# A two-block transformer on one core: five input transfers reordered, and a mixer's windowed means moved from VectorE to TensorE

## The chip, the cores and the metric

The kernel runs on one core of a Trainium2 chip. The metric is the time of one execution in device microseconds (us), the median of several runs. All data is fp32; TensorE does each fp32 matmul as two records of the profile ("x16" there is eight matmuls).

## What is computed

256 tokens of width 1024 (and 256 context tokens) pass through a first block of two layers and then a second block of two layers. The change touches two places: the very first norm (`rms_norm` of all 512 tokens with a modulation computed from `c`), and the mixer of each of the second block's two layers. There, one projection `u @ w_in` is split into attention (q, k, v), an indexer (qi, ki, wi) that selects keys, a gated convolution and a pooling:

```python
u = jnp.einsum('bsd,de->bse', a, w_in[i])
q, k, v, qi, ki, wi, u_conv, u_pool = jnp.split(u, IN_SPLITS, axis=-1)
y_attn = dsa_sparse_attention(q, k, v, qi, ki, wi)     # relu(qi.ki)*wi summed over 16 heads, top 64 keys
y_conv = conformer_conv(u_conv, ...)                   # 31 taps, layer norm, silu, 256x256 product
y_pool = multiscale_pool(u_pool, pool_w[i], pool_scale[i])
...
def multiscale_pool(u, pool_w, pool_scale):            # 4 groups of 64 columns, windows 2, 4, 8, 16
    for gi, w in enumerate(POOL_WINDOWS):
        win_sum = c[:, :, sl] - c_pad[:, POOL_PAD - w:POOL_PAD - w + S, sl]   # c: running sum over tokens
        outs.append(win_sum / count - uf[:, :, sl])    # causal mean minus the token itself
    y = jnp.einsum('bsgc,gcd->bsgd', y, pool_w)
    return y * pool_scale
```

## The kernel before

Every engine runs one straight program, written out stage by stage; semaphore counters order them. **Weights** are one stream of 128x128 blocks in the exact order of use, in chunks of 16 blocks (1 MB), which SyncE's queue loads into a ring of five chunks (`weight_ring`): a chunk is issued when the last use of the chunk five before it is done, and TensorE waits for a chunk's arrival once (`K.arrived`). `weight_blocks` lays the stream out, `next_blocks` books it.

**Start.** ScalarE's queue issues, in this order, the vectors, the tokens (`residual`, 2 MB), the first constants, `decay_rows` (32 numbers broadcast to 128 partitions) and `position_row` (256 integers broadcast). `have` waits for all of them. `first_norm` squares the eight token tiles on ScalarE (L666), TensorE sums them with a matrix of ones (L658), ScalarE takes the root (L668), VectorE the reciprocal (L680), multiplies (L683) and applies gain and shift (L691, with ScalarE's L675). Beside it TensorE computes the first modulation (L621) in eight steps, one chunk each: four before the sums, four behind. ScalarE's `rest_of_constants` then issues the other constants. The even mixer follows (L1877, L1885); `decay_rows` is read there at L1983 and L2069, and `position_row` only in the second block.

**Mixer of the second block (`sparse_mixer`).** TensorE projects 22 tiles one after another (`project(m)`, L2539, weights stationary; for wi and v the tokens are stationary, L2533), ping-pong between banks 0 and 1; ScalarE copies each out (`take`). Between tiles TensorE runs `rotate` (rotary products, L2545), `dots` (L2556), the sums of the layer norm (L2562, L2568), and at the end `small` (L2578 the convolution's product, L2582 the pooling's). VectorE's order is: `convolve` (L2685 to L2691), `pool_windows` (L2702 to L2709), rotary steps `rope(0)`, `rope(1)`, `centre`, `rope(2)`, two `add`, `rope(3)`, two `add`, `rope(4)`, four `add`, `select(0)`, `normalise`, `select(1)` (top-64 by repeated maximum), `rope(5)`, `rope(6)`, `rope(7)` (each L2717 to L2719). TensorE's `rotate(7)` waits for `rope(5)` because both use bank 7, and `small` stands behind it. The attention stage (first L761) waits for the masks, all rotary steps, v and `small`'s outcome (L2675, L2677); GpSimd's weight sums for the output projection wait for the same.

Of the kernel before, what the change touches and what calls it, by code (L numbers as in the profile page):

```python
# [16 lines left out]
ALU = mybir.AluOpType  # L17
# [75 lines left out]

def weight_blocks(x):
# [29 lines left out]
    for i in range(2):  # L124
# [3 lines left out]
        out.append(pack_tiles(w, columns(256, o[7])))  # L128
        out.append(pack_rows(w, [list(range(o[5], o[5] + 16)) + [-1] * 112]))
        out.append(pack_tiles(w, [list(range(o[4], o[4] + 64)) * 2]))  # L130
        out.append(pack_tiles(w, columns(1024, o[3])))
        out.append(pack_tiles(w, paired(0)))
        out.append(pack_tiles(w, columns(128, o[1])))
        out.append(pack_rows(w, columns(128, o[2])))
# [4 lines left out]
        out.append(np.stack([pool[:P, :P], pool[P:, P:]]))  # L139
        rows = np.concatenate([np.arange(512, 1024)] + [np.array(t) for t in paired(0)])  # L140
# [35 lines left out]
def constant_parts():  # L176
# [34 lines left out]
    w = np.array([2, 4, 8, 16])  # L211
    c["pool_count"] = np.stack([1.0 / np.minimum(t + 1, w[2 * n + (np.arange(P) // 64)][:, None]) for n in range(2)], 1)
# [432 lines left out]
def first_norm(K, h, piece, gains, gain, shift, out, tokens_ready, rest_of_constants):  # L645
# [1200 lines left out]
def even_projections(K, R, u, k_ready, qkvT, gate, qd, kvd, kpe, ktok, vtok, pads, conv, narrow, low_squares):  # L1846
# [109 lines left out]
    def scalar(act):  # L1956
# [25 lines left out]
        act.activation(narrow, ab[:, :, 64:96], ACT.Copy).then_inc(sg["e_narrow"].sem, 1)  # L1982
        act.activation(ea, R.rows[:, 0:16], ACT.Exp).then_inc(sg["e_rows"].sem, 1)  # L1983
# [49 lines left out]
    def vector(dve):  # L2033
# [34 lines left out]
        dve.tensor_scalar(x[:, :, 16:32], ab[:, :, 16:32], -1.0, None, ALU.mult)  # L2068
        dve.tensor_tensor(out=x[:, :, 0:16], in0=ab[:, :, 0:16], in1=bc(R.rows[:, 16:32], 1, 4), op=ALU.add).then_inc(sg["e_shifted"].sem, 1)  # L2069
# [406 lines left out]
def sparse_mixer(K, R, layer, u, deps, k_ready, ahead):  # L2476
# [9 lines left out]
    ppad = area.get(2, 16 + S)  # L2486
# [5 lines left out]
    sums = [area.get(2, 16 + S) for _ in range(4)]  # L2492
# [13 lines left out]
    needs = [8] + [tiles.index(("qi", i + 1)) + 1 for i in (0, 2, 4, 6)] + [tiles.index(("q", i + 1)) + 1 for i in (0, 2)] + [21]  # L2506
# [5 lines left out]
              "in_normed": 1, "in_active": 1, "in_small": 1, "in_small_out": 1, "in_masks": 1}  # L2512
    sg = {n: K.counter(n) for n in counts}
    at = {n: sg[n].reserve(c) for n, c in counts.items()}
    first = [K.next_blocks(KT, (sg["in_product"], at["in_product"] + m + 1)) for m in range(len(tiles))]
    small_first = K.next_blocks(6, (sg["in_small"], at["in_small"] + 1))

# [3 lines left out]
    def tensor(pe):  # L2521
        need(pe, deps)

        def project(m):
# [3 lines left out]
            if name in ("wi", "v"):  # L2528
# [41 lines left out]

        def small():
            pe.wait_ge(sg["in_active"].sem, at["in_active"] + 1)
            pe.wait_ge(sg["in_taken"].sem, at["in_taken"] + len(tiles))
# [11 lines left out]
        for m in range(len(tiles)):  # L2585
            project(m)
            if m == 12:
                rotate(0)
                rotate(1)
            elif m == 13:  # L2590
# [4 lines left out]
            elif m == 14:  # L2595
                dots(0)
                dots(1)
                pe.wait_ge(sg["in_centred"].sem, at["in_centred"] + 1)
                rotate(3)
            elif m == 15:  # L2600
                dots(2)
                dots(3)
                pe.wait_ge(sg["in_roped"].sem, at["in_roped"] + 3)
                variance()
            elif m == 16:
# [4 lines left out]
            elif m == 17:  # L2610
                dots(6)
                dots(7)
            elif m == 20:
                pe.wait_ge(sg["in_root"].sem, at["in_root"] + 1)
                rotate(5)
                pe.wait_ge(sg["in_roped"].sem, at["in_roped"] + 5)
                rotate(6)
        pe.wait_ge(sg["in_roped"].sem, at["in_roped"] + 6)
        rotate(7)
        small()  # L2620

    def scalar(act):
        act.wait_ge(sg["in_cleared"].sem, at["in_cleared"] + 1)

        def take(m):
# [7 lines left out]
            elif name == "p":  # L2633
                ins = act.activation(ppad[:, i, 16:], ps, ACT.Copy)
# [16 lines left out]
        for m in range(len(tiles)):  # L2651
            take(m)
            if m == 14:
# [4 lines left out]
            elif m == 15:  # L2658
                rectify(2)
                rectify(3)  # L2660
# [438 lines left out]
```

## Time and profile before

| | us |
|---|---|
| median of 3 runs | 2283.7 (2282.51 to 2284.52) |
| the profiled execution, own time | 2289.73 |
| its span, first to last instruction | 2287.6 |
| PE (TensorE matmul) busy | 2184.0 (95%) |
| PEld (TensorE weight load) busy | 1519.8 (66%) |
| DVE (VectorE) busy | 1061.5 (46%) |
| ACT (ScalarE) busy | 459.4 (20%) |
| POOL (GpSimd) busy | 139.7 (6%) |
| mean granted TensorE clock | 0.983 of full |
| read from HBM | 280.12 MB, 123 GB/s over the span |

Read it by stage: TensorE is busy nearly always, so what counts are the few places where it stands idle or runs at the lower clock. A granted clock of 1.00 is 2.4 GHz, 0.50 is 1.2 GHz.

### The profile page before, as it was taken

What the parts mean: (1) busy time and instruction counts of PE and PEld (TensorE: products, weight loads), DVE (VectorE), ACT (ScalarE), POOL (GpSimd) and SP (SyncE); (2) the same over time, 40 slices, a digit from 0 to 9 for tenths busy, and PEclk for the clock granted to TensorE, in tenths of its full rate; (3) what the DMA queues carried; (4) which work ended last, traced back from release to release, by engine and by line L of the source; (5) the groups of instructions that cost most, each with busy time, mean ns of one, the idle gap of its engine ahead of it and who ended that gap; (6) DMA issues with size and microseconds to landing.
All of it is one profiled execution on the core that took longest, in us unless ns stands there. A gap on an engine that the chain in (4) does not pass through costs nothing.

```text
span 2287.6 us, 33060 instructions
## 1 busy us (share of the span) xinstructions
PE 2184.0 (95%) x14140; PEld 1519.8 (66%) x14140; DVE 1061.5 (46%) x1902; ACT 459.4 (20%) x986; POOL 139.7 (6%) x158
## 2 busy tenths in 40 slices
PE   6999999999899999999999999998999999899998
PEld 3447878564588885466567884785785488668646
DVE  2575555461655446652453115675324428632443
ACT  2343211351200000131242000222210111311001
POOL 0003333000000000021100000002000000200000
PEclk9999999999999999999999999999999999999999
DMA  8221444402422224454113444332344433234442
GB/s 324 74 74 39 150 150 153 173 1 74 184 92 92 81 85 148 174 138 128 56 38 120 157 147 176 128 111 74 131 158 172 166 115 124 74 117 159 157 174 74
DMA packets 40799, 283.81 MB, mean 124 GB/s; under 512 B 4944, under 2 KB 6352, under 8 KB 7120
## 3 DMA queue, kind: packets, MB, share of 16 engines
q1 hardware_dynamic: 38480, 273.70, 33.0%
q0 software_dynamic: 1312, 3.15, 1.1%
q10 hardware_dynamic: 864, 4.87, 0.5%
q8 instruction: 113, 1.85, 0.3%
q14 instruction: 30, 0.25, 0.0%
HBM read 280.12 MB, written 1.05 MB: 123 GB/s over the span
## 4 chain that ended last, share of the span: by engine, by line
PE 89%; DVE 7%; ACT 2%; issue 1%; DMA 1%; ACTq 0%; DVEq 0%
PE banks L978 20%; PE banks L405 17%; PE banks L1389 12%; PE banks L1288 7%; PE banks L2539 6%; PE banks L1885 5%; PE banks L1568 2%; PE banks L1592 2%; PE banks L761 1%; PE banks L1588 1%; PE banks L621 1%; PE banks L443 1%; PE banks L776 1%; PE banks L493 1%; PE banks L767 1%
## 5 line engine op out<-in xcount | busy, mean ns | idle before, releaser
L405 PE MATMUL banks<-normed,weight_ring 128*128 128x256 f32 (+1 forms) x1280 | 294.9, 393 | 7.8 <-DVE normed L557 5.7
L405 PEld LDWEIGHTS banks<-normed,weight_ring 128*128 128x128 f32 x1280 | 244.9, 192 | 57.2 <-issue 15.3
L978 PE MATMUL banks<-arena 128*128 128x512 f32 x360 | 171.0, 593 | 0.7 <-DVE arena L1444 0.5
L1288 PE MATMUL banks<-normed,weight_ring 128*128 128x256 f32 x704 | 153.8, 382 | 3.4 <-ACT normed L571 3.4
L2539 PE MATMUL banks<-normed,weight_ring 128*128 128x256 f32 x640 | 151.4, 399 | 5.8 <-DVE normed L557 2.9
L1288 PEld LDWEIGHTS banks<-normed,weight_ring 128*128 128x128 f32 x704 | 134.8, 192 | 22.4 <-ACT normed L571 3.8
L978 PE MATMUL banks<-weight_ring,arena 128*128 128x512 f32 x322 | 149.2, 592 | 0.0
L2539 PEld LDWEIGHTS banks<-normed,weight_ring 128*128 128x128 f32 x640 | 128.0, 201 | 26.9 <-issue 4.6
L978 PEld LDWEIGHTS banks<-arena 128*128 128x128 f32 x360 | 68.2, 190 | 87.5 <-issue 86.1
L1885 PE MATMUL banks<-normed,weight_ring 128*128 128x512 f32 x288 | 126.1, 593 | 0.0
L978 PEld LDWEIGHTS banks<-weight_ring,arena 128*128 128x128 f32 x322 | 60.9, 190 | 73.1 <-issue 72.9
L3005 DVE TENSOR_TENSOR arena<-arena 128x256 f32<-128x256 f32 x64 | 27.2, 425 | 171.3 <-ACT arena L2993 170.6
L943 DVE TENSOR_TENSOR arena<-weight_ring 128x512 f32<-128x512 f32 x59 | 40.7, 690 | 141.1 <-PE banks L978 141.1
L1885 PEld LDWEIGHTS banks<-normed,weight_ring 128*128 128x128 f32 x288 | 54.3, 190 | 66.7 <-issue 66.7
L1389 PE MATMUL banks<-normed,weight_ring 128*128 128x256 f32 x352 | 82.9, 390 | 6.8 <-ACT normed L571 4.3
L1389 PEld LDWEIGHTS banks<-normed,weight_ring 128*128 128x128 f32 x352 | 68.8, 196 | 18.1 <-issue 5.1
L1441 DVE TENSOR_TENSOR arena<-squares,banks 128x512 f32<-128x512 f32 x22 | 15.1, 687 | 132.1 <-ACT squares L1417 132.1
L1015 ACT ACTIVATE branch<-banks 128x512 f32<-128x512 f32 x8 | 4.8, 598 | 336.6 <-PE banks L978 336.6
L1306 DVE TENSOR_TENSOR arena<-banks,arena 128x256 f32<-128x256 f32 x22 | 9.3, 424 | 131.4 <-PE banks L1288 127.1
L621 PE MATMUL banks<-weight_ring,silu_cond 128*32 128x512 f32 x384 | 54.2, 650 | 16.3 <-DMA weight_ring<-in_weights 7.3
L835 DVE TENSOR_REDUCE attention_small<-banks 128x1 f32<-128x512 f32 (+2 forms) x96 | 48.0, 530 | 45.5 <-PE banks L767 41.1
L815 ACT ACTIVATE arena<-banks,attention_small 128x512 f32<-128x512 f32 (+2 forms) x96 | 54.0, 563 | 60.3 <-DVE attention_small L835 60.3
(464 smaller groups left out, 3432.6 us busy)
## 6 DMA issues: line engine op xcount, KB each, us to landing
weight_ring<-in_weights SPq DMA_DIRECT2D x260, 1024.0 KB, 4.8
constants<-in_const ACTq DMA_DIRECT2D x1, 2209.5 KB, 13.9
residual<-in_tokens ACTq DMA_DIRECT2D x1, 2048.0 KB, 12.6
mix<-in_rpb POOLq DMA_DIRECT2D x32, 64.0 KB, 3.6
out<-residual SPq DMA_DIRECT2D x1, 1024.0 KB, 4.8
branch<-arena POOLq DMA_DIRECT2D x1, 512.0 KB, 4.9
normed<-in_ple POOLq DMA_DIRECT2D x1, 512.0 KB, 3.7
vector_params<-in_vectors ACTq DMA_DIRECT2D x1, 223.0 KB, 5.6
```

Of the source, the lines that this page charges most:

```text
L405: mm = pe.matmul(K.psum[lo:hi, banks[m % nb], 0:T], K.block(first[m] + k)[:, lo:hi], rhs(k), start=(k == 0), stop=(k == n_k - 1))
L621: mm = pe.matmul(o, self.silu[:, k, :], self.K.block(self.first[k] + 4 * j, 4), start=(k == 0), stop=(k == KT - 1))
L815: act.activation(prob[:, i % 4, 0:x.n], K.bank(i % 4, x.n), ACT.Exp, bias=maximum[:, i % 4:i % 4 + 1], accum_out=total[:, i % 4:i % 4 + 1] ...
L835: dve.reduce_max(maximum[:, i % 4:i % 4 + 1], K.bank(i % 4, rounds[r].n), AX, negate=True).then_inc(sg["maxima"].sem, 1)
L943: dve.tensor_tensor(out=t3, in0=b22, in1=b12, op=ALU.subtract)
L978: return pe.matmul(self.bank[i], left, b, start=(p == 0), stop=(p == n - 1))
L1288: mm = pe.matmul(K.bank(i % 4, T), K.block(first[i] + k), u[:, k, 0:T], start=(k == 0), stop=(k == KT - 1))
L1389: mm = pe.matmul(self.outs(p)[i], a[:, k * P:k * P + P], right(k), start=(k == 0), stop=(k == H - 1))
L1568: mm = pe.matmul(heads(2 * u)[halves[n], m, :], L[u][lv % 2][halves[n], m, :], X[u][halves[n], m, :], start=True, stop=True)
L1592: mm = pe.matmul(heads(2 * u + 1)[halves[n], m, :], PR[u][halves[n], m, :], Y[u][halves[n], m, :], start=True, stop=True)
L1885: mm = pe.matmul(K.bank(f % 4), K.block(first[f] + k), u[:, k, :], start=(k == 0), stop=(k == KT - 1))
L2539: mm = pe.matmul(K.bank(m % 2, S), K.block(first[m] + k), u[:, k, 0:S], start=(k == 0), stop=(k == KT - 1))
```

## The change

1. *Start.* `decay_rows` and `position_row` are issued behind the rest of the constants, and `have` counts two transfers fewer. ScalarE and VectorE wait for them (and all constants) before L1983 and L2069. The modulation's steps are split three before the sums and five behind.
2. *Pooling.* `pool_windows`, its padded tiles, their memsets and the constant `pool_count` go. The two p tiles are projected with tokens stationary, so that they come out by token, and TensorE multiplies them by banded 128x128 matrices (causal mean minus identity) that stand in the weight stream (`window_blocks`, 12 blocks a layer; the zero upper right block is not stored). ScalarE copies the result out.
3. *Order.* The p tiles move behind the qi tiles; `rotate`, `dots` and the layer norm's sums move to earlier tiles; `small` moves ahead of the v tile, so v moves behind the pooling's weights in the stream; `rope(5)` moves ahead of `select(1)`.

The stream has 262 chunks, not 260. The diff, cut to its core:

```diff
+def window_blocks():
+    i, j = np.arange(S)[:, None], np.arange(S)[None]
+    for w in (2, 4, 8, 16):
+        m = ((i <= j) & (i > j - w)) / np.minimum(j + 1, w) - (i == j)
+        out += [m[:P, :P], m[:P, P:], m[P:, P:]]
...
     def tensor(pe):                       # first_norm
-        piece.product(pe, 0, 4)
+        piece.product(pe, 0, 3)
...
-        piece.product(pe, 4, KT)
+        piece.product(pe, 3, KT)
...
+        need(act, K.constants_ready)
         act.activation(ea, R.rows[:, 0:16], ACT.Exp).then_inc(sg["e_rows"].sem, 1)
...
+        need(dve, K.constants_ready)
         dve.tensor_tensor(out=x[:, :, 0:16], in0=ab[:, :, 0:16], in1=bc(R.rows[:, 16:32], 1, 4), op=ALU.add)
...
-    tiles = [("a", 0), ("a", 1), ("g", 0), ("g", 1), ("p", 0), ("p", 1), ("wi", 0), ("ki", 0)] + [("qi", i) for i in range(8)] \
+    tiles = [("a", 0), ("a", 1), ("g", 0), ("g", 1), ("wi", 0), ("ki", 0)] + [("qi", i) for i in range(8)] + [("p", 0), ("p", 1)] \
         + [("q", i) for i in range(4)] + [("k", 0), ("v", 0)]
...
-            if name in ("wi", "v"):
+            if name in ("wi", "v", "p"):
...
+        def windows():
+            pe.wait_ge(sg["in_taken"].sem, at["in_taken"] + tiles.index(("p", 1)) + 1)
+            pe.wait_ge(sg["in_relu"].sem, at["in_relu"] + 8)
+            for g in range(4):
+                rows, m = slice(64 * (g % 2), 64 * (g % 2) + 64), g // 2
+                o = K.psum[rows, 5, m * S:m * S + S]
+                for at_block, (t, lo, stop) in enumerate(((0, 0, True), (0, P, False), (1, P, True))):
+                    K.arrived(pe, window_first + 3 * g + at_block)
+                    mm = pe.matmul(o[:, lo:lo + P], ptok[:, m, t, rows], K.block(window_first + 3 * g + at_block), start=(at_block < 2), stop=stop)
+            mm.then_inc(sg["in_meaned"].sem, 1)
...
+            elif m == 19:                 # scalar
+                act.wait_ge(sg["in_meaned"].sem, at["in_meaned"] + 1)
+                act.activation(z.rearrange("p m n -> p (m n)"), K.bank(5), ACT.Copy).then_inc(sg["in_pool"].sem, 1)
...
         convolve()
-        pool_windows()
         rope(0)
...
         normalise()
+        rope(5)
         select(1).then_inc(sg["in_masks"].sem, 1)
-        rope(5)
         rope(6)
...
         def rest_of_constants(act):
-            act.dma_start(K.const[:, n_first:], const[:, n_first:]).then_inc(constants_loaded.sem, 16)
+            for dst, src in ((K.const[:, n_first:], const[:, n_first:]), (R.rows, rows.to_broadcast([P, 32])), (R.positions, positions.to_broadcast([P, S]))):
+                act.dma_start(dst, src).then_inc(constants_loaded.sem, 16)
-        have = [(loaded, 16 * 4)] + have_vectors
+        have = [(loaded, 16 * 2)] + have_vectors
```

TensorE at the end of a mixer, before: the last three projected tiles by weights (q2, q3, k), `rotate(5)` and `rotate(6)`, v, `rotate(7)`, and `small` ahead of the attention.

```order
L2539 MATMUL banks<-normed,weight_ring 128x256 x24
L2545 MATMUL banks<-arena,constants 128x256 x4
L2533 MATMUL banks<-weight_ring,normed 128x128 x16
L2545 MATMUL banks<-arena,constants 128x256
L2578 MATMUL banks<-branch,weight_ring 128x256 x4
L2582 MATMUL banks<-branch,weight_ring 128x256 x2
L761 MATMUL banks<-arena 128x128 x2
```

The same place after the change; L2592 is `windows`, L2601 and L2605 are `small`, L2546 is v.

```order
L2558 MATMUL banks<-arena,constants 128x256 x2
L2552 MATMUL banks<-normed,weight_ring 128x256 x8
L2592 MATMUL banks<-weight_ring,arena 64x128 x12
L2552 MATMUL banks<-normed,weight_ring 128x256 x8
L2558 MATMUL banks<-arena,constants 128x256 x2
L2601 MATMUL banks<-branch,weight_ring 128x256 x4
L2605 MATMUL banks<-branch,weight_ring 128x256 x2
L2546 MATMUL banks<-weight_ring,normed 128x128 x16
L2558 MATMUL banks<-arena,constants 128x256
L770 MATMUL banks<-arena 128x128 x2
```

`small` now stands ahead of v and of the last rotary product, and twelve window matmuls are new.

VectorE around `normalise`, before: the end of `select(0)`, the reciprocal and product of `normalise`, then the first step of `select(1)`.

```order
L2750 TENSOR_SCALAR arena<-arena 128x128
L2751 TENSOR_TENSOR arena<-arena,constants 128x128
L2742 RECIPROCAL inverses<-roots 128x256
L2743 TENSOR_TENSOR branch<-branch,inverses 128x512
L2748 MAX arena<-arena 128x8
```

After the change, at the same place:

```order
L2764 TENSOR_SCALAR arena<-arena 128x128
L2765 TENSOR_TENSOR arena<-arena,constants 128x128
L2756 RECIPROCAL inverses<-roots 128x256
L2757 TENSOR_TENSOR branch<-branch,inverses 128x512
L2731 TENSOR_TENSOR arena<-banks,mix 128x512
L2732 TENSOR_TENSOR arena<-arena,mix 128x512
L2733 TENSOR_TENSOR arena<-arena 128x512
L2762 MAX arena<-arena 128x8
```

The three instructions of `rope(5)` have come in ahead of `select(1)`.

## Rows read from the trace of the kernel before

**Rows 1.** Waits of PE, second mixer (1800 to 1990 us): waiting line <- releaser: us, times, longest

```profile
PE banks L2545 <- DVE arena L2719: 6.8, 1, 6.8
```

**Rows 2.** The chain, 0 to 130 us: start, us, what

```profile
2.89 20.19 DMA position_row<-in_positions
...
23.10 0.64 ACT normed L666
...
23.79 8.94 PE banks L658 x16
...
43.11 11.45 PE banks L1877 x64
...
76.38 0.36 PE banks L1898 x4
```

**Rows 3.** DMA issues, 0 to 80 us: size, us from issue to landing

```profile
constants<-in_const ACTq DMA_DIRECT2D x1, 2209.5 KB, 13.9
...
constants<-in_const ACTq DMA_DIRECT2D x1, 128.5 KB, 15.0
```

**Rows 4.** Timeline, 0 to 130 us: start, us, what, idle before

```profile
1.67 0.45 ACTq L2839 DMA_DIRECT2D constants<-in_const  x1
...
16.51 1.93 PE L621 MATMUL banks<-weight_ring,silu_cond 128*32 128x512 f32 x8 [0.94 <-DMA weight_ring<-in_weights]
...
32.64 3.64 PE L621 MATMUL banks<-weight_ring,silu_cond 128*32 128x512 f32 x32
...
37.00 0.66 PE L634 MATMUL banks<-constants,roots 128*128 128x128 f32 x4 [0.72 <-ACT roots L629]
...
56.25 0.21 ACT L1983 ACTIVATE gates<-decay_rows 128x16 f32<-128x16 f32 x1
...
66.00 0.23 DVE L2074 SCALAR_TENSOR_TENSOR gates<-gates 128x64 f32<-128x64 f32 x1
```

**Rows 5.** Stretches: us, PE, PEld, DVE, ACT, POOL busy; clock, DMA, GB/s

```profile
30.00:32.00 2.00, 2.00 (x6) 0.93 (x5) 0.00 (x0) 0.00 (x0) 0.00 (x0) 1.00 0.98 410
...
48.00:50.00 2.00, 2.00 (x12) 2.00 (x11) 0.00 (x0) 0.00 (x0) 0.00 (x0) 0.50 0.96 398
...
200.00:400.00 200.00, 192.52 (x5302) 160.11 (x5302) 106.44 (x165) 40.76 (x67) 78.33 (x70) 1.00 0.37 136
```

**Rows 6.** Timeline of PE, first mixer of the second block

```profile
1471.98 4.38 PE L2533 MATMUL banks<-weight_ring,normed 128*128 128x16 f32 x32
...
1541.42 3.73 PE L2533 MATMUL banks<-weight_ring,normed 128*128 128x128 f32 x32
1551.91 1.22 PE L2545 MATMUL banks<-arena,constants 128*128 128x256 f32 x2 [6.76 <-DVE arena L2719]
...
1559.01 0.49 PE L761 MATMUL banks<-arena 64*128 64x128 f32 x4 [1.51 <-ACT mix L2677]
```

**Rows 7.** The chain, same mixer: tile pitch, `small`, a 64-column product

```profile
1476.36 23.42 PE banks L2539 x96
...
1501.08 3.45 PE banks L2539 x16
...
1553.14 3.41 PE banks L2578 x8
...
1561.54 0.37 PE banks L785 x4
```

**Rows 8.** Timeline of DVE, same mixer

```profile
1494.67 0.72 DVE L2702 TENSOR_TENSOR branch<-arena 128x542 f32<-128x542 f32 x1
...
1499.41 0.69 DVE L2709 TENSOR_TENSOR branch<-branch,arena 128x512 f32<-128x512 f32 x1
...
1540.71 0.69 DVE L2743 TENSOR_TENSOR branch<-branch,inverses 128x512 f32<-128x512 f32 x1
...
1549.51 0.43 DVE L2751 TENSOR_TENSOR arena<-arena,constants 128x256 f32<-128x256 f32 x1
...
1554.73 0.42 DVE L2719 TENSOR_TENSOR arena<-arena 128x256 f32<-128x256 f32 x1
```

More of the change, by code:

```diff
@@ L131, in weight_blocks @@
         out.append(pack_tiles(w, columns(1024, o[3])))
+        out += [pack_rows(w, columns(128, o[7] + 128 * j)) for j in range(2)]
         out.append(pack_tiles(w, paired(0)))
+        out.append(window_blocks())
         out.append(pack_tiles(w, columns(128, o[1])))
-        out.append(pack_rows(w, columns(128, o[2])))
         out.append(pack_tiles(x["conv_pw_2"][i], columns(256)))
@@ L139, in weight_blocks @@
         out.append(np.stack([pool[:P, :P], pool[P:, P:]]))
+        out.append(pack_rows(w, columns(128, o[2])))
         rows = np.concatenate([np.arange(512, 1024)] + [np.array(t) for t in paired(0)])
@@ L2491, in sparse_mixer @@
     acc, xc = area.get(2, S), area.get(2, S)
-    sums = [area.get(2, 16 + S) for _ in range(4)]
     z = area.get(2, S)
@@ L2505, in sparse_mixer @@
     whole = [ki] + [qi[:, i:i + 2, :] for i in (0, 2, 4, 6)] + [q[:, i:i + 2, :] for i in (0, 2)] + [kk]
-    needs = [8] + [tiles.index(("qi", i + 1)) + 1 for i in (0, 2, 4, 6)] + [tiles.index(("q", i + 1)) + 1 for i in (0, 2)] + [21]
+    needs = [6] + [tiles.index(("qi", i + 1)) + 1 for i in (0, 2, 4, 6)] + [tiles.index(("q", i + 1)) + 1 for i in (0, 2)] + [21]
     turn_bank = [2, 7, 7, 2, 2, 7, 2, 7]
@@ L2511, in sparse_mixer @@
               "in_added": 8, "in_conv": 1, "in_pool": 1, "in_mean": 1, "in_centred": 1, "in_squared": 1, "in_variance": 1, "in_root": 1,
-              "in_normed": 1, "in_active": 1, "in_small": 1, "in_small_out": 1, "in_masks": 1}
+              "in_normed": 1, "in_active": 1, "in_small": 1, "in_small_out": 1, "in_masks": 1, "in_meaned": 1}
     sg = {n: K.counter(n) for n in counts}
     at = {n: sg[n].reserve(c) for n, c in counts.items()}
-    first = [K.next_blocks(KT, (sg["in_product"], at["in_product"] + m + 1)) for m in range(len(tiles))]
+    first = [K.next_blocks(KT, (sg["in_product"], at["in_product"] + m + 1)) for m in range(20)]
+    window_first = K.next_blocks(12, (sg["in_meaned"], at["in_meaned"] + 1))
+    first.append(K.next_blocks(KT, (sg["in_product"], at["in_product"] + 21)))
     small_first = K.next_blocks(6, (sg["in_small"], at["in_small"] + 1))
+    first.append(K.next_blocks(KT, (sg["in_product"], at["in_product"] + len(tiles))))
     def dot_banks(i):
@@ L2694, in convolve @@
             ins.then_inc(sg["in_conv"].sem, 1)
-        def pool_windows():
-            dve.wait_ge(sg["in_taken"].sem, at["in_taken"] + 6)
-            prev = ppad
-            for n, s in enumerate(sums):
-                w = 1 << n
-                lo = 2 * w - 1
-                step(dve.tensor_tensor(out=s[:, :, lo:], in0=prev[:, :, lo:], in1=prev[:, :, lo - w:16 + S - w], op=ALU.add))
-                prev = s
-            count = K.c("pool_count").rearrange("p (m n) -> p m n", m=2)
-            for n, s in enumerate(sums):
-                rows, m = slice(64 * (n % 2), 64 * (n % 2) + 64), n // 2
-                ins = dve.tensor_tensor(out=z[rows, m, :], in0=s[rows, m, 16:], in1=count[rows, m, :], op=ALU.mult)
-            step(ins)
-            dve.tensor_tensor(out=z, in0=z, in1=ppad[:, :, 16:], op=ALU.subtract).then_inc(sg["in_pool"].sem, 1)
         def rope(j):
```

60 lines of the change are left out of this document (28 added, 32 removed).

## The prediction

> **What bounds the kernel now.** I read the page first: TensorE is busy 95% of the span, so the kernel can only gain where TensorE stands idle, runs at the lower clock, or loses work. Then I read, for the two places that the change touches, the chain of waits, and behind it each engine's timeline.
>
> At the start the chain runs through a transfer: `position_row` is issued at 2.89 us, takes 20.19 and so lands at 23.08, and ScalarE's first square starts at 23.10 [rows 2]. The reader should see that what ScalarE needs is there earlier: the first constants are issued at 1.67 [rows 4] and land 15.0 later [rows 3], at 16.67, and the tokens were issued ahead of them. The last 6.4 us are spent on two transfers that nobody reads before 55 us. From the squares on, the chain is fixed work: TensorE's sums from 23.79 to 32.73, then root, reciprocal, multiplies and gains until TensorE starts the even mixer at 43.11 [rows 2].
>
> In each mixer of the second block TensorE works through until v is done (1541.42 + 3.73 = 1545.15), waits 6.76 us for `rope(5)` on VectorE, does `rotate(7)` and `small`, and waits 1.51 us for `small`'s copies; the attention starts at 1559.01 [rows 6]. The second mixer has the same wait of 6.8 us [rows 1]. A hidden third cost stands beside them: behind the wait TensorE runs slowly. The eight records of the convolution's product take 3.41 us, 0.43 each, where the same shape takes 3.45 / 16 = 0.216 in the projections [rows 7]; that is the 1.2 GHz level.
>
> **The start, step by step.** With the two transfers gone from `have`, the squares start at 16.7. TensorE ends the third modulation step at 16.51 + 1.93 = 18.44 [rows 4]; the first square (0.64) is done at 17.3, so the sums start at 18.4, not 23.79: this is why one step was moved behind them. The sums took 8.94 us. At 0.43 for each of 16 records of 512 columns (twice 0.216) they would be 6.9, so before they ran partly at the lower level, after TensorE had been nearly idle. Now they follow 1.93 us of work directly. I take 8.4, with 7.4 and 9.4 as bounds: the end is at 26.8 (25.8 to 27.8) against 32.73, 5.9 us earlier.
>
> The modulation must not become the later of the two paths. Its five remaining steps at 3.64 / 4 = 0.91 us [rows 4] end at 31.4, if chunk 7 is there: eight chunks and 2.4 MB of vectors, tokens and constants are 10.8 MB, and the queue moves 410 GB/s [rows 5], which puts it near 28.5. Before, the copy and the turn took from 32.64 + 3.64 = 36.28 to 37.00 + 0.66 = 37.66 [rows 4], 1.4 us; now they end at 32.8. VectorE's eight multiplies end at about 35.9, so there are 3 us to spare, and the even mixer starts at 43.11 - 5.9 = 37.2. Its first product (64 records, 11.45 us, 0.18 each [rows 2]) ran mostly at 1.2 GHz (granted clock 0.50 at 48 to 50 us [rows 5]) after 5.45 us of idling; now the idling is 4.4 us, and I leave this as it is. Were it all at the upper level, at the 0.117 of v's records below, it would give 4 us more.
>
> What is paid for it: ScalarE and VectorE now wait, ahead of L1983 and L2069, for all constants. These are issued near 32 and land 13.9 us later or somewhat more [rows 3] (one chunk more competes, 0.26 MB of `pool_count` less), at 46 to 48. The two small transfers behind them took 6.4 us before, so they land between 47 and 54. ScalarE comes to L1983 at 56.25 - 5.9 = 50.4. Queued behind it on both engines is the way to the decays, 9.9 us long (56.25 to 66.23 [rows 4]), which TensorE reads at 76.38 [rows 2], now 70.5. Up to 60 the landing costs nothing.
>
> That transfers of 16 and 128 KB take 6.4 us is as the Trainium skill says in "DMA: Bandwidth & Descriptors", Queues, rings and completion order: each engine goes round between its queues packet by packet, so a small transfer waits behind the weights' large packets. The trace agrees (6.4 us for 0.14 MB). By this rule the two meet the weights again in their new place, which is the rival of the late constants below.
>
> **The mixer, step by step.** VectorE loses the pooling, 1494.67 to 1500.10 [rows 8], 5.4 us, and `rope(5)` goes ahead of `select(1)`, which lasts from 1541.40 to 1549.94 [rows 8], 8.5 us. Before, `rope(5)` ended at 1551.9. Now it ends at 1543.4 even if the 5.4 us are all lost in waiting, and near 1538 to 1540 otherwise. Some are lost: VectorE is done with `rope(1)` near 1498, but the mean that `centre` needs stands on TensorE behind thirteen tiles and three rotary products, which end at 1501.08 as before [rows 7]. TensorE reaches `rotate(7)` at 1550.8 (next paragraph), so its wait is gone. What is late next is not VectorE but TensorE's own queue.
>
> I count that from v's end. In front of it come now:
> twelve window matmuls, 24 records of 128 columns on 64 columns of the array. The trace has such records in the attention, four in 0.37 us, 0.093 each [rows 7], and full-width ones in v, 32 in 3.73, 0.117 each [rows 6]. So 2.2 to 2.8; I take 2.5, between the two.
> The two p tiles in v's form: 3.73 - 3.45 = 0.28 each, 0.56.
> `small`, 12 records at 0.216, 2.6.
> The sum is 5.7: v ends at 1545.15 + 5.7 = 1550.8. Then `rotate(7)`, 0.43, and `rope(7)` on VectorE, three instructions of 0.42 [rows 8] and the handover, 1.35, ahead of the attention: 1552.6. The copies of `small` and of the means hide under v (3.73). Against 1559.01 that is 6.4 us. Told as a difference: 6.76 + 1.51 of waits and 2.6 of slow clock (the 14 records from 1551.91 to 1557.50 take 5.6, not 3.0) go, 2.5 + 0.56 of work and 1.35 of a new wait come.
> Two mixers give 12.8; the step to `rope(7)` is handed over on three engines, so I take 12.6.
>
> Bounds. If VectorE won nothing from the dropped sums, `rope(6)` would end as before near 1553.9 and `rope(7)` at 1555.1: 3.9 us a mixer, 7.8 in all. Upwards, windows at the 0.093 and a clock that is never lowered give 7 us, 14 in all.
>
> Free of cost: two chunks more (0.8% of the stream), since the queue can move 410 GB/s [rows 5] and moves 123 on the mean; four fewer memsets on GpSimd, which waits over 100 us; the copy of the means on ScalarE, 0.6 us, beside k's 3.45. If the cover of k were gone it would cost 0.6.
>
> The Trainium skill, "TensorEngine Tiling (Array Packing)", Key Properties, says that changing the tiling mode drains TensorE, which speaks against windows between full-width products. In the attention the trace changes between full-width and 64-column products several times per microsecond, and four such records still take 0.37 us [rows 7]; by the rows a switch costs nothing that shows, by the rule the windows would cost some tenths of a microsecond more, within the 2.8 above.
>
> **The sum.** 5.9 + 12.6 = 18.5 us. The profiled execution took 2289.73 us around a span of 2287.6, so its successor should have a span of 2269.1. The median of the runs is 6.0 lower than the profiled execution; the differences carry over: 2283.7 - 18.5 = 2265.2.
>
> **The rivals.**
> *The mixers give about half* (3.9 us each). For it: VectorE waits for `centre`, and every later step of it is fed by TensorE in a denser order. Against it: `rope(6)` may come up to 2.8 us later than I place it before `rope(7)` notices. 2283.7 - 5.9 - 7.8 = 2270.0.
> *TensorE falls to 1.2 GHz behind the windows*, as it did in its 16-column stage (4.38 us [rows 6]): the six tiles behind it took 23.42, not 6 x 3.45 = 20.7 [rows 7]. Price 2.7 a mixer, 5.4: 2270.6. Against it: long stretches of 64-column products are granted 1.00 (200 to 400 us [rows 5]).
> *The start gives little*, because chunks 3 to 7 come late or the sums run wholly at the lower level (13.8 us, end at 32.2). Then only 0.5 to 3 us are won: about 2269.5.
> *The clock is kind*: the even mixer's first product at the upper level, 4 us more, 2261.
> *Slower: late constants.* The place is the wait ahead of L1983; ScalarE and VectorE stand behind it. It costs nothing until 60 us and then one for one; for the kernel to be slower than before, they would have to land after 60 + 18.5 = 78.5, more than 46 us after their issue, against 13.9 before. Price at 80 us: 2285.
> *The change does not do what it says*, in that VectorE is not what TensorE waits for. The row names it (6.76 <-DVE arena L2719), and the start's wait names the transfer; I leave nearly nothing to it.
>
> **How the numbers follow.** The forecast with its own bounds (2262 to 2268.5) 0.66; half in the mixers 0.11; the clock behind the windows 0.06; little at the start 0.07; kind clock 0.06; late constants 0.02; nothing done 0.02. The range leaves out the last two and the outer parts of the others: 2260 to 2271. A difference under 0.2% (4.6 us) could not be told from none by this measurement; all cases but the last two are beyond it, and a mix of the small ones might fall into it: faster 0.94, same 0.04, slower 0.02.
>
> **What would show it.** Right: ScalarE's first square near 16.7, its releaser the first constants or the tokens; TensorE's sums ending near 27 and the even mixer's start near 37; no `pool_windows` on VectorE; no wait of 6.8 us in the mixers but one of about 1.4 on the last rotary step ahead of the attention; `small` at 0.216 a record; the stage from the mixer's first tile to the attention about 103 us, not 109.5. Wrong: a new wait of TensorE for VectorE inside the mixer (at `dots` or `rotate(6)`), a granted clock under 1 behind the windows, a wait of L1886 or of the modulation for `weight_ring`, or ScalarE idle ahead of L1993 beyond 60 us.

## The result, and the profile after

| | median us | lowest to highest |
|---|---|---|
| before | 2284.11 | 2282.51 to 2286.11 (4 runs) |
| after | 2255.85 | 2253.83 to 2256.64 (4 runs) |

The ratio is 0.9878, with a 95% interval of 0.9865 to 0.9890: 28.3 us faster, by the interval 25 to 31. The forecast was 18.5 us, 2265.2, with a range from 2260: the direction was right, and the forecast gain a third too small. The profiled execution took 2256.64 us around a span of 2254.8, with a mean granted clock of 0.990.

First the start. The chain of waits of after, 0 to 130 us (start, us, what):

```profile
16.62 1.93 PE banks L630 x8
18.55 8.37 PE banks L667 x16
...
31.05 4.90 DVE normed L692 x8
...
37.30 11.21 PE banks L1886 x64
```

The timeline of ScalarE shows why, with the releaser of the first square in the bracket, and where the three late transfers went:

```profile
16.81 4.26 ACT L675 ACTIVATE normed<-residual 128x512 f32<-128x512 f32 x8 [9.74 <-DMA constants<-in_const]
...
31.41 0.35 ACTq L2851 DMA_DIRECT2D constants<-in_const  x1
31.80 0.51 ACTq L2851 DMA_DIRECT2D decay_rows<-in_rows  x1
32.34 0.47 ACTq L2851 DMA_DIRECT2D position_row<-in_positions  x1
...
50.20 0.21 ACT L1993 ACTIVATE gates<-decay_rows 128x16 f32<-128x16 f32 x1
```

No transfer of `position_row` stands in the chain of [rows 2] any more. The even mixer starts at 37.30 instead of 43.11.

Then the mixer. The timeline of TensorE, first mixer of after (start, us, what, idle before):

```profile
1442.79 14.05 PE L2552 MATMUL banks<-normed,weight_ring 128*128 128x256 f32 x64 [2.92 <-DVE normed L566]
1456.68 3.64 PE L2546 MATMUL banks<-weight_ring,normed 128*128 128x16 f32 x32
1460.17 17.51 PE L2552 MATMUL banks<-normed,weight_ring 128*128 128x256 f32 x80
...
1525.69 1.80 PE L2592 MATMUL banks<-weight_ring,arena 128*64 128x128 f32 x24
1527.42 3.72 PE L2552 MATMUL banks<-normed,weight_ring 128*128 128x256 f32 x16
1530.98 1.03 PE L2558 MATMUL banks<-arena,constants 128*128 128x256 f32 x4
1531.84 1.89 PE L2601 MATMUL banks<-branch,weight_ring 128*128 128x256 f32 x8
1533.57 1.03 PE L2605 MATMUL banks<-branch,weight_ring 128*128 128x256 f32 x4
1534.43 3.73 PE L2546 MATMUL banks<-weight_ring,normed 128*128 128x128 f32 x32
1538.00 0.60 PE L2558 MATMUL banks<-arena,constants 128*128 128x256 f32 x2
1540.05 0.49 PE L770 MATMUL banks<-arena 64*128 64x128 f32 x4 [1.45 <-DVE arena L2733]
```

The wait of 6.76 of [rows 6] is gone, the convolution's product in `small` takes 1.89 for eight records instead of 3.62 in the same view of before (its row stands below; [rows 7] counts 3.41 of it on the chain), and what is left is a wait of 1.45 for the last rotary step. From the first tile (1442.79) to the attention (1540.05) are 97.26 us. In the profile of before this was 109.51, and my sum made it 103.1 (1552.6 - 1449.5).

**The kernel before a second time.** So the new mixer came as drawn, yet 6 us shorter. The run with the start alone, told below, came first, and its mixers, in which nothing is changed, took 106.5 us and not 109.5. So I profiled the kernel before, unchanged, once more (`before_again`).

> The kernel before, unchanged, one more profiled execution. Chance theory (the first profile, at 2289.73, was an execution in which TensorE's clock was low at unlucky moments, and my sum was taken from it): about 2284, mixers of about 106.5 us as in the kernel with the start alone, full clock at their first tile and behind wi. Typical theory (the first profile shows what usually happens): 109.5 and 110.8 us again.

It took 2280.91 us, span 2279.1. The timeline of TensorE, same mixer:

```profile
1446.11 20.96 PE L2539 MATMUL banks<-normed,weight_ring 128*128 128x256 f32 x96 [2.92 <-DVE normed L557]
...
1498.26 1.13 PE L2545 MATMUL banks<-arena,constants 128*128 128x256 f32 x4 [0.92 <-DVE arena L2719]
...
1545.06 1.22 PE L2545 MATMUL banks<-arena,constants 128*128 128x256 f32 x2 [6.78 <-DVE arena L2719]
1546.08 3.62 PE L2578 MATMUL banks<-branch,weight_ring 128*128 128x256 f32 x8
...
1552.58 0.49 PE L761 MATMUL banks<-arena 64*128 64x128 f32 x4 [1.51 <-ACT mix L2677]
```

And of the execution on which the prediction was built:

```profile
1449.50 22.64 PE L2539 MATMUL banks<-normed,weight_ring 128*128 128x256 f32 x96 [2.92 <-DVE normed L557]
...
1476.20 23.58 PE L2539 MATMUL banks<-normed,weight_ring 128*128 128x256 f32 x96
...
1505.23 1.03 PE L2545 MATMUL banks<-arena,constants 128*128 128x256 f32 x4
```

The same program, the same six tiles: 22.48 us from start to start there (1471.98 - 1449.50), 20.79 here; `wi` 4.22 and 3.49; the six tiles behind it 23.42 and 20.81. Together 5.0 us of lower clock stood in the execution I read and not in the other. The two waits at the end, 6.8 and 1.51, are there in both. The mixer is 106.47 us long in `before_again`, not 109.51.

In `before_again` something else shows behind the wait. Stretches of both kernels from the attention's first record on (us, busy times, clock, DMA share, GB/s), before, then after:

```profile
1552.50:1560.00 7.50, 7.42 (x42) 5.54 (x44) 2.41 (x10) 4.17 (x16) 6.99 (x7) 0.60 0.33 131
```

```profile
1540.00:1548.00 8.00, 7.95 (x65) 5.89 (x66) 2.79 (x14) 4.06 (x21) 7.52 (x8) 1.00 0.59 246
```

Behind the waits the clock is low not only in `small`: it is low again at the attention's head, which gets through 42 records in 7.5 us instead of 65 in 8. After the change the attention starts at the upper level. So I divide the profiles at five points: TensorE's first product of the even mixer (column "start"), the first tile of the first mixer, the attention's first record, and the same two in the second mixer. The entries are differences of two such starts in a timeline of TensorE, the last one up to the end of the span; "clock" is the mean granted over the span. The changes to the kernels are told further down.

| profile | start | to mixer 1 | mixer 1 | behind it | mixer 2 | behind it | span | clock |
|---|---|---|---|---|---|---|---|---|
| before | 43.11 | 1406.4 | 109.5 | 309.0 | 110.8 | 308.8 | 2287.6 | 0.983 |
| before_again | 43.56 | 1402.5 | 106.5 | 310.2 | 106.3 | 310.0 | 2279.1 | 0.988 |
| before_wi_wide | 44.18 | 1402.9 | 106.6 | 310.3 | 106.4 | 310.0 | 2280.3 | 0.986 |
| start_only | 36.65 | 1404.4 | 106.5 | 310.3 | 106.4 | 310.0 | 2274.2 | 0.985 |
| no_sums | 43.69 | 1409.4 | 104.2 | 309.0 | 104.1 | 308.8 | 2279.2 | 0.987 |
| rope5_only | 43.84 | 1406.3 | 102.3 | 311.2 | 102.3 | 312.5 | 2278.5 | 0.987 |
| order_only | 37.30 | 1404.6 | 100.8 | 308.7 | 100.8 | 308.6 | 2260.7 | 0.992 |
| mixers_only | 44.10 | 1406.6 | 97.3 | 309.0 | 97.3 | 308.8 | 2263.0 | 0.991 |
| after | 37.30 | 1405.5 | 97.3 | 308.9 | 97.3 | 308.6 | 2254.8 | 0.990 |

The column "to mixer 1" is work that no kernel here changes, and it runs from 1402.5 to 1409.4: by so much two profiles differ where nothing was done, and so their spans are not simply compared. Undisturbed before (`before_again`) against after: start 6.3, mixers 9.2 and 9.1, behind them 1.3 and 1.4, in all 27.3 us, for a measured 28.3. The 1.3 and 1.4 are not in every execution with the old end of the mixer: three profiles show them (310), `before` and `no_sums` don't (309).

The column behind the mixer holds two effects. In `before_again` the output projection's first product comes 22.74 us after the attention's first record, in after 19.86: the slow head costs 2.9 us. Then 1.6 are given back. The next block begins behind a wait of 2.87 us in both, and behind it the clock fell in after (and in `before`), but not in `before_again`. The stretches from that block's first product on, after and then `before_again`:

```profile
1594.90:1604.90 10.00, 9.98 (x39) 8.56 (x40) 3.58 (x9) 0.77 (x2) 0.00 (x0) 0.84 0.09 13
```

```profile
1610.30:1620.30 10.00, 9.98 (x46) 8.76 (x47) 3.59 (x9) 0.77 (x2) 0.00 (x0) 1.00 0.18 54
```

### The profile page after: what moved, and what is told of

Same layout as the page of the kernel before. It is cut to its first block, busy times and chain, and to the rows that moved or that the text cites. A ratio compares the mean times of both kernels' runs of the same rounds, so it can differ in the third digit from the quotient of the medians.

```text
span 2254.8 us, 33258 instructions
## 1 busy us (share of the span) xinstructions
PE 2171.7 (96%) x14252; PEld 1512.5 (67%) x14252; DVE 1051.4 (47%) x1884; ACT 461.0 (20%) x988; POOL 139.0 (6%) x148
## 4 chain that ended last, share of the span: by engine, by line
PE 92%; DVE 4%; ACT 2%; issue 1%; DMA 1%; SPq 0%; ACTq 0%; DVEq 0%
PE banks L987 20%; PE banks L414 18%; PE banks L1398 12%; PE banks L1297 7%; PE banks L2552 6%; PE banks L1894 5%; PE banks L1577 2%; PE banks L1601 2%; PE banks L630 2%; PE banks L770 2%; PE banks L1597 1%; PE banks L502 1%; PE banks L2546 1%; PE banks L452 1%; PE banks L785 1%
## 5 line engine op out<-in xcount | busy, mean ns | idle before, releaser
L414 PEld LDWEIGHTS banks<-normed,weight_ring 128*128 128x128 f32 x1280 | 244.9, 192 | 56.9 <-issue 15.3
L1297 PE MATMUL banks<-normed,weight_ring 128*128 128x256 f32 x704 | 153.9, 382 | 3.4 <-ACT normed L580 3.4
L1297 PEld LDWEIGHTS banks<-normed,weight_ring 128*128 128x128 f32 x704 | 134.8, 192 | 22.5 <-ACT normed L580 3.8
L2552 PE MATMUL banks<-normed,weight_ring 128*128 128x256 f32 x576 | 127.5, 381 | 5.8 <-DVE normed L566 2.9
L2552 PEld LDWEIGHTS banks<-normed,weight_ring 128*128 128x128 f32 x576 | 108.6, 190 | 22.7 <-issue 5.0
L1894 PEld LDWEIGHTS banks<-normed,weight_ring 128*128 128x128 f32 x288 | 54.3, 190 | 66.7 <-issue 66.7
L1398 PE MATMUL banks<-normed,weight_ring 128*128 128x256 f32 x352 | 83.9, 393 | 6.7 <-ACT normed L580 4.3
L1398 PEld LDWEIGHTS banks<-normed,weight_ring 128*128 128x128 f32 x352 | 68.8, 197 | 19.0 <-issue 5.1
L3002 ACT ACTIVATE arena<-banks 128x256 f32<-128x256 f32 x64 | 24.5, 383 | 205.7 <-PE banks L414 205.7
```

The source lines that it names most:

```text
L414: mm = pe.matmul(K.psum[lo:hi, banks[m % nb], 0:T], K.block(first[m] + k)[:, lo:hi], rhs(k), start=(k == 0), stop=(k == n_k - 1))
L1297: mm = pe.matmul(K.bank(i % 4, T), K.block(first[i] + k), u[:, k, 0:T], start=(k == 0), stop=(k == KT - 1))
L1398: mm = pe.matmul(self.outs(p)[i], a[:, k * P:k * P + P], right(k), start=(k == 0), stop=(k == H - 1))
L1894: mm = pe.matmul(K.bank(f % 4), K.block(first[f] + k), u[:, k, :], start=(k == 0), stop=(k == KT - 1))
L2552: mm = pe.matmul(K.bank(m % 2, S), K.block(first[m] + k), u[:, k, 0:S], start=(k == 0), stop=(k == KT - 1))
```

## The experiments

**Start and mixers apart.** `start_only` is before with the first item of the change, `mixers_only` with the other two.

> The changes to the start alone, mixers as before. Sum theory (my prediction's terms hold, and what came beyond them is TensorE's clock in the mixers, which depends on the moment at which a thinly filled stage comes and not on its neighbours): 5.8 us faster than before, 2278.3, the even mixer starting near 37.3; the clock in the mixers may differ from before although nothing in them is changed. Order theory (the lower clock went because wi now stands behind g and not behind p): 2278.3 as well, but both mixers keep 1.2 GHz behind wi and last 109.5 to 110.8 us as before.

> The pooling by products and the new order, start as before. Sum theory: each mixer 6.4 us shorter by waits and work, plus 0.7 for windows that took 1.8 and not 2.5, plus up to 5 where the clock is not lowered at wi and at the first tile: 2262 to 2270, and in some profile a mixer with 1.2 GHz behind wi. Order theory: no mixer has it, each lasts about 97.3, 2261.

`start_only` took 2278.41 us, ratio 0.9968 (0.9955 to 0.9981), 5.9 less than the 2284.29 of before beside it. `mixers_only` took 2264.58, ratio 0.9910 (0.9895 to 0.9925), 19.7 less. The two add up to 25.6 of 28.3, within the intervals. So the start's 5.9 was right, and the 12.6 of the mixers was the wrong term: the runs give it 17 to 24.

**Is the lower clock at the mixer's head caused by the 16-column stage?** My rival had read it so. `wi` over 128 columns instead of 16, in both kernels (the columns beyond 16 are not used):

```diff
-                w = 16 if name == "wi" else P
+                w = P
```

> The kernel before, with wi's matmuls over all 128 columns of its block and not 16 (the other 112 are zeros and go unread), so that the stage is filled. Both theories: wi takes 3.7 instead of 4.2 us and the tile behind it 3.45 instead of 6.15, 3.2 us a mixer, 6.4 in all, 2277.7, if wi's clock was lowered in every run of before; less by the share of runs in which it was not (sum theory: 2278 to 2282).

> The changed kernel with the same widening of wi. Order theory: the clock is not lowered there anyway, wi takes 3.73 instead of 3.49, 0.5 us slower, 2256.3. Sum theory: the runs in which the moment is unlucky lose nothing now, so 0.5 slower in some and up to 6 faster in others, on the mean 0 to 3 faster.

Before so changed: 2284.37, ratio 0.9999 (0.9989 to 1.0008); mixers of 106.6 and 106.4. After so changed: 2257.74, ratio 0.9876 (0.9860 to 0.9893); mixers of 97.26. Widening changes nothing in either that these runs can tell. `before_again` says the same: with 16 columns, the stage ran at the upper level there too. And in `before` the six tiles ahead of the stage were slow already (22.48 us against 20.79). Where the level falls at the mixer's head differs from execution to execution. `early_last` below has both in one profile: the head of mixer 1 at the upper level, and mixer 2 with a granted clock of 0.82 from 1850 to 1872 us and of 0.88 from 1872 to 1896, 102.9 us long instead of 96.5.

The Trainium skill, "TensorE: Matmul & The Clock Gate", Part 1, says that the number of slow products at a kernel's start differs between runs of the same kernel. The trace agrees, and shows it in the middle of a kernel too: 22.48 and 20.79 us for the same 96 records.

**What in the mixer made the 9.2 us?** `order_only` is after with the pooling on VectorE again, where it was (p tiles ahead of `wi`, the sums between `convolve` and `rope(0)`), and with everything else in its new place among the qi and q tiles.

```diff
-    tiles = [("a", 0), ("a", 1), ("g", 0), ("g", 1), ("wi", 0), ("ki", 0)] + [("qi", i) for i in range(8)] + [("p", 0), ("p", 1)] \
+    tiles = [("a", 0), ("a", 1), ("g", 0), ("g", 1), ("p", 0), ("p", 1), ("wi", 0), ("ki", 0)] + [("qi", i) for i in range(8)] \
...
         convolve()
+        pool_windows()
         rope(0)
```

> The changed kernel with the pooling as VectorE's sums again and p projected ahead of wi as before; the new places of the rotary products, the dots, small, v and rope(5) stay. Order theory (the wait goes because rope(5) and the dots come earlier, and VectorE's own waits would have covered most of the 5.4 us of sums): the mixer takes 95.5 to 97.5 us against 97.26, so 2252 to 2257. Removal theory (the 5.4 us off VectorE are what is won): 97.26 + 5.4 = 102.7, 2266.7.

2262.92 us, ratio 0.9912 (0.9894 to 0.9930), mixers of 100.75: between the two expectations, so both were off. Its waits of TensorE, 1440 to 1560 us (waiting line, releaser: us, times, longest):

```profile
PE banks L771 <- DVE arena L2732: 4.6, 1, 4.6
PE banks L2552 <- DVE normed L567: 2.9, 1, 2.9
PE banks L2558 <- ACT arena L2650: 2.2, 1, 2.2
```

The order, as far as `order_only` has it, is worth 5.7 us a mixer. VectorE, still with its sums, then makes the attention wait 4.6 us for `rope(7)`. The step from here to after gives the other 3.5, and it is not the sums alone: the two p tiles move as well. With p ahead, the layer norm's mean (L2575) stands 53.3 us into the mixer (1495.18 - 1441.89), with p behind 46.4 (1489.17 - 1442.79), and VectorE's `centre` waits for it 2.35 and 0.79 us, `order_only` first and then after:

```profile
1496.32 0.76 DVE L2750 SCALAR_TENSOR_TENSOR branch<-banks,arena 128x256 f32<-128x256 f32 x2 [2.35 <-PE banks L2575]
```

```profile
1490.32 0.75 DVE L2751 SCALAR_TENSOR_TENSOR branch<-banks,arena 128x256 f32<-128x256 f32 x2 [0.79 <-PE banks L2575]
```

How the 3.5 us divide between the two, no run here shows.

`no_sums` asks the reverse: the old order, and VectorE's sums left out (`z` is one add of p with itself, so the pooling is not computed).

```diff
-            for n, s in enumerate(sums):
-                step(dve.tensor_tensor(out=s[:, :, lo:], in0=prev[:, :, lo:], in1=prev[:, :, lo - w:16 + S - w], op=ALU.add))
...
-            dve.tensor_tensor(out=z, in0=z, in1=ppad[:, :, 16:], op=ALU.subtract).then_inc(sg["in_pool"].sem, 1)
+            dve.tensor_tensor(out=z, in0=ppad[:, :, 16:], in1=ppad[:, :, 16:], op=ALU.add).then_inc(sg["in_pool"].sem, 1)
```

> The kernel before, its order unchanged, with VectorE's pooling sums left out: z is one add of p with itself, so the pooling is not computed. VectorE loses about 4.7 us of work a mixer. Theory A (VectorE alone sets the end of the undisturbed mixer): mixer 106.4 - 4.7 = 101.7 us, kernel 2284 - 9.4 = 2274.7. Theory B (VectorE is fed late by ScalarE and TensorE, 5.7 and 2.6 us of its waits lie in the mixer, and they take up part of the work removed): mixer 103 to 104.5, kernel 2277 to 2280.

2278.75, ratio 0.9978 (0.9967 to 0.9990); mixers of 104.16 and 104.07, 2.3 less than in `before_again`, as theory B had it. Of the 2.3, `rotate(7)` comes 1.6 earlier (1550.50 - 1453.11 = 97.39 us after the first tile, not 98.95), and the rest is that `small` was sooner at the upper level in this profile. So 1.6 of VectorE's 4.7 us come through. Its timeline shows where the others went:

```profile
1498.90 0.42 DVE L2706 TENSOR_TENSOR arena<-banks,mix 128x256 f32<-128x256 f32 x1 [1.62 <-PE banks L2545]
...
1504.09 0.76 DVE L2726 SCALAR_TENSOR_TENSOR branch<-banks,arena 128x256 f32<-128x256 f32 x2 [1.92 <-PE banks L2562]
```

VectorE gets there earlier and waits 1.62 and 1.92 us for TensorE, where `before_again` waited only 0.50 (at L2717, directly behind `centre`). In the old order two thirds of the sums' time, 3.0 of 4.7 us, are lost in waiting. The prediction had described such a loss, at `centre`, for the new order. What is left of the gain, 1.6 us, is less than the 3.5 in the new order, where the p tiles make room too.

**The moved rotary step by itself.**

```diff
         normalise()
+        rope(5)
         select(1).then_inc(sg["in_masks"].sem, 1)
-        rope(5)
```

> The kernel before with one statement moved on VectorE: rope(5) ahead of select(1). Theory A (the wait of 6.8 us is that of rope(5) behind select(1), and VectorE's remaining queue, rope(6) and rope(7), ends later by nothing): TensorE's wait goes, the end is then set by select(1), rope(6) and rope(7) on VectorE: mixer about 102.3 us (-4.1), kernel about 2276. Theory B (VectorE's whole queue sets the end and order inside it is worth nothing): mixer stays at 106.4, TensorE's wait only moves to behind small, kernel 2284.

The mixers are 102.29 and 102.28, as theory A said to the tenth. The whole kernel gives 3.3 us, 2280.59 (ratio 0.9983, 0.9973 to 0.9993), not 8. The waits of TensorE, 1440 to 1560 us, say why:

```profile
PE banks L761 <- DVE arena L2719: 6.8, 1, 6.8
```

and the stretches that follow:

```profile
1552.50:1560.00 7.50, 7.50 (x36) 5.61 (x38) 2.37 (x9) 2.78 (x15) 7.14 (x7) 0.50 0.00 0
1560.00:1580.00 20.00, 19.83 (x145) 13.12 (x142) 8.95 (x25) 9.85 (x35) 5.71 (x5) 0.96 0.01 1
```

The wait has not gone but moved, from ahead of `rotate(7)` to directly ahead of the attention, and now all of the lower clock behind it falls on the attention: 36 records in 7.5 us. (In `order_only` 4.6 us of waiting stand there; the granted clock over the 7.5 us behind is 0.77, and the attention's head takes 1.4 us longer than in after.) "Behind it" reads 311.2 and 312.5 instead of 310.2 and 310.0, so 1.0 and 2.5 us of the 8.2 won in the mixers are given back: 4.7 are left by the profiles, and 3.3 by the runs, whose interval goes from 1.6 to 6.2.

**The new tail put back.** `old_tail` is after with v ahead of `small` and `rope(5)` behind `select(1)` again.

```diff
-                small()
                 pe.wait_ge(sg["in_roped"].sem, at["in_roped"] + 6)
                 rotate(7)
+        small()
...
-        rope(5)
         select(1).then_inc(sg["in_masks"].sem, 1)
+        rope(5)
```

> The changed kernel with the end of the mixer as before: v ahead of small, small behind rotate(7), rope(5) behind select(1); the products for the pooling and the earlier dots stay. Count by engines: rope(5) would end at 90.7 us of the mixer, TensorE comes to rotate(7) at 92.5, so no wait of 6.8; small and its copies then stand open ahead of the attention, about 96.7 to 97.3 us, 2255 to 2256. Tail theory (moving rope(5) and small is what is won): 8.5 us later on VectorE, a wait of 4 or more on TensorE, 101 to 104 us, 2263 to 2269.

2257.11, ratio 0.9876 (0.9860 to 0.9892), mixers of 97.31 and 97.32. Its one wait at the end of the mixer:

```profile
PE banks L770 <- ACT mix L2705: 1.5, 1, 1.5
```

The new tail trades a wait of 1.5 us for the copies of `small` against one of 1.45 for `rope(7)`. With the sums gone and the products earlier, `rope(5)` is early enough in either place.

**The last wait taken too.** `early_last` is after with `rotate(7)` behind `small` and ahead of v.

```diff
-        pe.wait_ge(sg["in_roped"].sem, at["in_roped"] + 6)
-        rotate(7)
+                pe.wait_ge(sg["in_roped"].sem, at["in_roped"] + 6)
+                rotate(7)
```

> The changed kernel with rotate(7) directly behind small and ahead of v, so that rope(7) on VectorE lies beside v's matmuls. By my present theory (the end of a mixer is now set by TensorE's own queue plus the handover of the last rotary step, 1.45 us of wait ahead of the attention) that wait goes and nothing takes its place: mixer 96.1 instead of 97.26 us, twice, 2253.6 us. Rival: VectorE is not ready for rotate(7) that early (rope(6) ended at 1535.51, small ends at 1534.43), so TensorE waits about 1 us ahead of v instead: mixer 97.2, no change to 2255.85.

Mixer 1 is 96.48 us long; the wait of 1.45 became one of 0.7 (L770 <-ACT arena L2665, the copy of v), which I had not counted. Mixer 2 fell to the lower level at its head. TensorE's timeline, first tile and first rotary products of mixer 1, then of mixer 2:

```profile
1445.51 14.05 PE L2552 MATMUL banks<-normed,weight_ring 128*128 128x256 f32 x64 [2.92 <-DVE normed L566]
...
1480.24 1.46 PE L2558 MATMUL banks<-arena,constants 128*128 128x256 f32 x6
...
1851.02 17.11 PE L2552 MATMUL banks<-normed,weight_ring 128*128 128x256 f32 x64 [2.92 <-issue]
...
1892.16 1.46 PE L2558 MATMUL banks<-arena,constants 128*128 128x256 f32 x6
```

The way to the rotary products takes 34.73 and 41.14 us, 6.4 more, and the whole mixer is 6.4 us longer: in the new order what the clock costs at the head arrives in full at the attention. The median of 2256.55 (ratio 0.9885, 0.9866 to 0.9904) is not told from after's 2255.85. A gain of 0.8 us a mixer, 1.6 in all, lies under what these runs can tell.

**The start, two details.** `four_steps` puts four modulation steps ahead of the sums, as before, not three. `unwaited` issues the two small transfers at their old early place, but signals them on the late constants' semaphore, so that nothing at the start waits for them.

```diff
+            for dst, src in ((R.rows, rows.to_broadcast([P, 32])), (R.positions, positions.to_broadcast([P, S]))):
+                act.dma_start(dst, src).then_inc(constants_loaded.sem, 16)
```

> The changed kernel with four modulation steps ahead of the sums again, not three. By my sum: the fourth step waits for its chunk until about 19.5 and ends near 21.5, so the sums start 3 us later, 2258.9. Rival: the sums run more at the upper clock because TensorE was busy before, and only 1 to 2 us are lost, 2257.5.

> The changed kernel with the two small transfers (decay_rows, position_row) issued at their old early place, but signalled on the late constants' semaphore, so that nothing at the start waits for them. If the gain at the start came from no longer waiting for them, the time is that of the changed kernel (2255.85), the first square near 9.7 to 10 us and TensorE's sums ending near 26.9. Rival: their place in the queue delayed the weights or the tokens: the sums end up to 1 us or more later, 2257 or above.

`unwaited`: 2256.87, ratio 0.9881 (0.9866 to 0.9896), first square at 17.01, sums' end at 26.52, start 36.90. It was the wait for the two transfers that cost 6 us, not their place in the queue. (The 9.7 to 10 us of the expectation are the idle time ahead of the first square, not its start, which stands above at 16.81.) `four_steps`: 2257.86, ratio 0.9892 (0.9873 to 0.9912). Its chain:

```profile
2.13 17.00 DMA weight_ring<-in_weights
...
19.18 1.94 PE banks L630 x8
21.11 8.27 PE banks L667 x16
...
39.77 11.16 PE banks L1886 x64
```

The fourth step waits for a chunk that lands at 19.13, and the even mixer starts at 39.77, 2.5 us later than after. The medians are 2.0 apart, with intervals that overlap; the profile is the better witness here.

## Why the direction was right and the size wrong

**The start** held step by step. The squares start at 16.81 (16.7), the sums end at 26.92 (26.8), the even mixer starts at 37.30 (37.2). The term was 5.9, and the runs gave 5.9. The late constants cost the kernel nothing, as argued: the last of the three transfers lands at 49.9 (47 to 54), VectorE waits 0.70 us for it (L2080), ScalarE's L1993 is at 50.20 (50.4), and TensorE does not wait.

**The drawing of the mixer** held too: VectorE no longer waited for inside the mixer, a wait of 1.45 (forecast 1.35) on the last rotary step, `small` at the upper level. The windows were taken at 2.5 us, from 2.2 to 2.8; their 24 records took 1.80, 0.075 each, less than the lower bound.

**The step that failed** is the sentence "The median of the runs is 6.0 lower than the profiled execution; the differences carry over". It takes the 6.0 for something that stands equally in before and after, and so leaves the mixers' term at 12.6, taken from the profiled execution. By the stages that term is 18.3 (9.2 and 9.1), by the runs of `mixers_only` 19.7. The spans of `before` and `before_again` differ by 8.5 us: 7.5 stand in the mixers, of which 2.4 are given back behind them, and 3.9 stand in the stretch ahead. My sum went "v ends at 1545.15 + 5.7 = 1550.8", and 1545.15 holds 5.0 us of lower clock at the mixer's head.

In before this is partly hidden. In `before_again` TensorE comes to the layer norm's mean 4.8 us earlier in the mixer than in `before`, but then waits 0.92 us for VectorE, which it doesn't in `before`; at the next rotary products 3.6 are left, at `rotate(7)` 3.5, behind a wait of 6.8 in both, and at the attention 3.0, since in `before` the clock came back sooner in `small`. So 5.0 us of clock change that mixer by only 3.0 (109.51 to 106.47). After the change TensorE itself sets the end, and such a loss counts in full, as mixer 2 of `early_last` shows (6.4 of 6.4). I kept the 5.0 in the sum as fixed work and so made the new mixer 103.1 long. Take them off, and 0.7 for the windows: 97.4, and 97.26 was measured. Against the undisturbed 106.4 that is 9.1 a mixer, and not 6.3.

So the two executions of the kernel before differed not by a constant but in who waits for whom. The six tiles of [rows 7] in 23.42 us, against 20.7 at the usual pitch, were in front of me. I priced them as a rival (the chip falls to 1.2 GHz behind the windows) and did not ask whether the same tiles are slow in every execution. Both wide variants and `before_again` show that they are not. Nor is the slow head a property of the old kernel: `early_last` has it in the new order.

**The term that was missing:** the lower clock behind TensorE's wait. I charged it to `small` alone (2.6 us). In three of five profiles with the old end it comes back at the attention's head too, 2.9 us of which 1.6 are given back further on, so 1.3 to 1.4 us a mixer, 2.7 in all. `rope5_only` shows the same cost, larger (2.3 and 3.9 us against the 308.9 and 308.6 of after), where the wait stands directly ahead of the attention.

Together: 18.3 in place of 12.6 is 5.7 more, and behind both mixers up to 2.7, which with the 18.5 gives 24.2 to 26.9; measured are 28.3, by the interval 25 to 31. The last 1.4 us or more I can't place; the stretch that nobody changed moves by more than that from profile to profile. One thing stays open with it: the three profiles with mixers of 106.4 (`before_again`, `start_only`, `before_wi_wide`) come from executions 2.0 to 3.0 us faster than the medians of their kernels. How often a mixer's head is slow in the executions without a profile, in either kernel, no run here shows.

**Which part earned what.** A mixer of 106.4 us: the new order with the old sums 100.8; the old order without the sums 104.1; both, with the products, 97.26. The sums' absence is worth 2.3 in the old order (1.6 of it without the clock's part). In the new one, moving the pooling to TensorE is worth 3.5, with the new place of the p tiles and the products' 2.4 us of TensorE's time in it. The place of `small`, v and `rope(5)` is worth nothing measurable once the rest is in.

## What to carry to other kernels

One profile is one execution: where it is slower than the median of the runs, find where the difference lies before taking sums from it. An identical stage that takes 23.4 us in one place and 20.8 in another is the sign, and a part of it hidden behind another engine's wait comes out in full in a sum that removes the wait. Work taken off an engine that is fed late turns in part into waiting, until its feeders are moved earlier: order and offload were worth 5.7 and 2.3 alone, and 9.1 together. And a wait of 7 us on TensorE cost more than its length here, so a wait that is only moved next to dense work is paid again.

## What the runs showed of the hardware

- Behind TensorE's wait of 6.8 us the clock was low in `small` (3.62 us for eight records, 1.89 at the upper level), and in three of five profiles again at the attention's head (granted 0.60 over 7.5 us); where the attention followed the wait of 6.8 directly it was 0.50, behind one of 4.6 it was 0.77. The attention's head took 2.9, 3.7 to 3.9 and 1.4 us longer. Where only a wait of 1.45 us stood ahead of it, the granted clock stayed at 1.00.
- Behind the same wait of 2.87 us in unchanged work, the clock was 0.84 over 10 us in one execution and 1.00 in another, worth 1.6 us.
- Where the clock fell at the head of a mixer differed between executions of one program, and between two identical mixers of one execution (96.5 and 102.9 us).
- Products on 64 columns of the array between full-width tiles took 0.075 us a record, and the tile behind them 3.72 us, where such tiles take 3.62 to 3.72 elsewhere in the same timeline: no cost for the switch shows.
